# Strassen products of an FFN: 512- and 256-column matmuls in another order, the second kind two k tiles behind the first

## What is computed

```python
def swiglu(h, w_in, w_out):
    a, b = jnp.split(h @ w_in, 2, axis=-1)
    return (jax.nn.silu(a) * b) @ w_out
# h: 512 x 2048, w_in: 2048 x 2*D_FF, D_FF = 5632, all float32
```

## Time and profile before

| | |
|---|---|
| time of the kernel, median of 3 runs | 2776.76 us (2773.27 to 2780.72) |
| the profiled execution's own time | 2771.05 us |
| its span in the profile | 2769.2 us |
| PE busy | 2729.6 us, 99% of the span |
| DVE busy | 2170.0 us, 78% |
| ACT busy | 1140.6 us, 41% |
| granted TensorE clock, mean | 0.997 of full speed |

### The profile page before, as it was taken

The page is one execution under the profiler, slowest core; times in us unless marked ns, Lnnn a source line. Parts: engine busy times, 40 slices in busy tenths (PEclk is TensorE's granted clock), DMA queues, the critical chain, the costliest instruction groups (busy, mean ns, idle before and its releaser), DMA issues.

```text
span 2769.2 us, 39539 instructions
## 1 busy us (share of the span) xinstructions
PE 2729.6 (99%) x15566; PEld 2311.8 (83%) x15566; DVE 2170.0 (78%) x2984; ACT 1140.6 (41%) x1697; POOL 368.5 (13%) x540
## 2 busy tenths in 40 slices
PE   7999999999999999999999999999999999999997
PEld 2688888888888888888888888888888888998996
DVE  6555775987885685676789999999999887877877
ACT  4332333223443532222245555555555554453541
POOL 0001331001333110001100111111111111000001
PEclk9999999999999999999999999999999999999999
DMA  9736885345775645767644444444443336434432
GB/s 403 325 95 148 196 188 144 116 129 191 231 226 180 239 134 182 247 210 269 231 149 145 156 145 149 145 152 144 150 153 125 124 112 217 140 91 148 138 103 96
DMA packets 144540, 475.27 MB, mean 172 GB/s; under 512 B 24993, under 2 KB 29489, under 8 KB 140130
## 3 DMA queue, kind: packets, MB, share of 16 engines
q1 hardware_dynamic: 85858, 301.43, 33.6%
q0 software_dynamic: 49760, 157.67, 18.1%
q10 hardware_dynamic: 8736, 13.63, 1.4%
HBM read 428.14 MB, written 44.44 MB: 171 GB/s over the span
## 4 chain that ended last, share of the span: by engine, by line
PE 92%; DMA 3%; DVE 2%; ACT 2%; issue 0%; SPq 0%; ACTq 0%; POOL 0%; DVEq 0%
PE ps L2831 19%; PE ps L2535 12%; PE ps L2537 12%; PE ps L2536 12%; PE ps L2833 10%; PE ps L2882 3%; PE ps L2881 3%; PE ps L2880 3%; PE ps L2859 2%; PE ps L2860 2%; PE ps L2861 2%; PE ps L2552 2%; DMA ada_mix<-in_w_ac 1%; PE ps L2514 1%; PE ps L2579 1%; PE ps L2621 1%
## 5 line engine op out<-in xcount | busy, mean ns | idle before, releaser
L1407 DVE TENSOR_TENSOR hw_lo<-hw_raw,hw_hi 128x1024 fp32r<-128x1024 f32 x220 | 269.3, 1224 | 318.8 <-ACT hw_hi L868 317.6
L868 ACT ACTIVATE hw_hi<-hw_raw 128x1024 fp32r<-128x1024 f32 x220 | 232.7, 1059 | 674.6 <-DMA hw_raw<-in_w_in 458.3
L2831 PE MATMUL ps<-t_hi_lo,wx_hi 128*128 128x512 f32 x1312 | 412.0, 395 | 0.0
L2103 DVE TENSOR_TENSOR wx_lo<-wx,wx_hi 128x1024 fp32r<-128x1024 f32 x287 | 351.3, 1224 | 41.4 <-ACT wx_hi L1261 36.9
L2535 PE MATMUL ps<-h_hi,hw_hi 128*128 128x512 f32 x896 | 354.0, 395 | 0.0
L2537 PE MATMUL ps<-h_hi,hw_lo 128*128 128x512 f32 x896 | 349.4, 390 | 0.0
L2536 PE MATMUL ps<-h_lo,hw_hi 128*128 128x512 f32 x896 | 348.7, 389 | 0.0
L1261 ACT ACTIVATE wx_hi<-wx 128x1024 fp32r<-128x1024 f32 x287 | 302.8, 1055 | 104.8 <-PE ps L2833 98.9
L2831 PE MATMUL ps<-h_hi_lo,wx_hi 128*128 128x512 f32 x984 | 309.0, 395 | 0.0
L2833 PEld LDWEIGHTS ps<-t_hi_lo,wx_lo 128*128 128x128 f32 x1312 | 246.5, 188 | 58.3
L2833 PE MATMUL ps<-t_hi_lo,wx_lo 128*128 128x256 f32 x1312 | 257.7, 278 | 0.0
(11 more groups left out here) (429 smaller groups left out, 5672.6 us busy)
## 6 DMA issues: line engine op xcount, KB each, us to landing
wx<-in_w_fi SPq DMA_DIRECT2D x164, 512.0 KB, 3.6
hw_raw<-in_w_in SPq DMA_DIRECT2D x128, 512.0 KB, 4.6
ada1m<-in_w_ar POOLq DMA_DIRECT2D x96, 512.0 KB, 4.6
ada_mix<-in_w_ac SPq DMA_DIRECT2D x16, 2048.0 KB, 15.3
dw<-in_w_fo SPq DMA_DIRECT2D x80, 384.0 KB, 3.1
ada1g<-in_w_ar POOLq DMA_DIRECT2D x32, 512.0 KB, 5.2
hw_raw<-in_w_glu SPq DMA_DIRECT2D x32, 512.0 KB, 4.6
hw_raw<-in_w_out SPq DMA_DIRECT2D x32, 512.0 KB, 4.3
```

Source lines behind the costliest of these rows:

```text
L868: act.activation(hw_hi[slot(n)][:, :], hw_raw[slot(n)][:, :], ACT.Copy).then_inc(w_hi, 1)
L1407: tt(hw_lo[s][:, :], hw_raw[s][:, :], hw_hi[s][:, :].bitcast(F32), SUB).then_inc(w_lo, 1)
L2103: tt(wx_lo[b][:, :], wx[b][:, :], wx_hi[o % 4][:, :].bitcast(F32), SUB).then_inc(w_lo, 1)
L2831: mm(out[:, :], wh[:, P * k:P * k + P], both[:, :, k, :], start=opens and k == 0, stop=False, skip_group_check=True)
```

## The change

Before, a product's matmuls stand in groups of two k tiles: two wide, two narrow, and so on. After, the wide matmul of k tile k is followed by the narrow one of k tile k - 2: a product begins with three wide ones, wide and narrow then take turns, and it ends with three narrow ones. No matmul is added or removed and none changes its operands; the waits ahead of the product and the count at its end stay. The order of the additions into a bank is another.

```diff
                 pe.wait_ge(w_lo, N_W + o + 1)
-                for k0 in range(0, ST, 2):
-                    for k in (k0, k0 + 1):
+                for k in range(ST + 2):
+                    if k < ST:
                         mm(out[:, :], wh[:, P * k:P * k + P], both[:, :, k, :], start=opens and k == 0, stop=False, skip_group_check=True)
-                    for k in (k0, k0 + 1):
-                        ins = mm(out[:, 0:CW], wl[:, P * k:P * k + P], xh[:, k, :], start=False, stop=k == ST - 1, skip_group_check=True)
+                    if k >= 2:
+                        ins = mm(out[:, 0:CW], wl[:, P * (k - 2):P * (k - 1)], xh[:, k - 2, :], start=False, stop=k == ST + 1,
+                                 skip_group_check=True)
                 ins.then_inc(w_used, 1)
```

## The result

Over 20 executions of each, the changed kernel took 2781.27 us in the median (2776.14 to 2784.58), the kernel before 2776.12 us (2772.62 to 2781.59). The ratio is 1.0017, with a 95% interval of 1.0011 to 1.0023: 4.7 us slower, clear of the noise and within the 0.3% that the prediction called no change.

What follows compares the result with a forecast made beforehand. TensorE's unbroken matmul sequence was taken as the bound. Couples in turn plus the runs of three gave -2.9 to +6.7 us, +5.5 at 7 to 1, discounted to +4 on 2776.8: 2780.8 us, range 2771 to 2790.

Steps and rivals of the forecast that it cites:

- The bound: Stage of the change, 1491 to 2291 us: TensorE's own matmul sequence sets its length, PE busy all 800.00 us without waiting.
- The size: Whole kernel: +4 us on the median of 2776.8, giving 2780.8 us.
- Five couples in turn, at one of two speeds: Middle of each product: alternating couples at 346.7 or 353.3 ns each, 1733 to 1767 ns for five, 1762 at 7 to 1.
- The share of 7 in 8: Couples in turn in units_by_k and u_half: 7 in 8 ran at 353.3 ns, used to weight the two speeds.
- Three wide and three narrow at 1043.3 ns: Product's start and end: 1040 ns at the unmixed pace plus 3.3 ns for one round trip between the kinds.
- The discount by a quarter: Whole stage: three quarters of +5.5 us taken, +4 us, since the three wide ones restart the sequence in every product.
- The sign that was named in line 2831's length: Wide matmuls of the stage: mean length would rise above 395 ns, towards 397, if turns are slow.
- The weight loads, priced at nothing: Stage: exactly one load lies under each matmul in either order, so the new order costs nothing in load time.
- Free mixing: Rival, 20%: couples in turn run as in u_half's last unit; stage -2.9 us, kernel 2773.9 us.
- The state in which every couple costs 360 ns: Rival, 17%: every turn in the stage is a long one; stage +16 us, kernel 2793 us.
- Cheap narrow ones at 340 ns a couple: Rival, 5%: narrow matmuls slip in at 113 ns behind wide ones; stage 13.4 us less, kernel 2763 us.

Runs made afterwards that it cites:

- e1: Kernel before, each product's eight wide matmuls first, then all eight narrow ones: stage 801.66 us against 799.76, kernel 1.0009 of the kernel before.
- e4: Kernel before, products in the order WWWNNWWWNNNWWNNN (W wide, N narrow), three round trips between the kinds: stage 801.68 us against 799.76.
- e7: Kernel before, wide and narrow in strict turn, narrow matmuls of 192 columns instead of 256: stage 780.61 us.
- e2: Kernel before, wide and narrow matmuls in strict turn from the first k tile: stage 811.24 us against 799.76, kernel 1.0040 of the kernel before.
- e6: Kernel before, wide and narrow in strict turn, narrow matmuls of 384 columns instead of 256: stage 933.70 us.
- e8: Kernel before, with the 16 small matmuls of power_rows one unit of u_half earlier: stage 799.762 us as before, but TensorE waited 5.59 us at them.

## Why the prediction was right, point by point

- **The bound.** Right: TensorE's own sequence sets the stage, before and after, and no wait of PE turned up in it. The loss of 4.5 us is all busy time.
- **The size.** +4 us on the median was forecast; the medians give +5.2, the ratio +4.7 and the stage +4.5. The stage fell within the 796.9 to 806.5 us that were named for it.
- **Five couples in turn, at one of two speeds.** Right in kind: the changed kernel has both, 346.7 ns in one product of three and 351 to 352.5 in the others. Cut as the prediction cut them, from the first narrow matmul to the three last ones, five couples took 1735, 1751 and 1764 ns in the three products of the cycle, 1750 on average, where 1762 was reckoned. The share of 7 in 8 for the slow one was no property of the code. It counted one execution; over 13 traces the fast one is the more frequent in the first three units of u_half.
- **Three wide and three narrow at 1043.3 ns.** This step failed. It took 3.3 ns for a round trip, from four of them costing 13.3, as if each had a price that adds. e1 measured 20 ns for one, and e4 20 for three. In the changed kernel the three wide and three narrow took 1049 to 1055 ns, 1052 on average (in the rows above 0.70 + 0.35 us): 9 ns too few were reckoned here, 12 too many for the couples, and the discount took off another 5. That the sum came out near the measured one (2800.5 after the discount, 2802.2 measured) is luck in that part.
- **The discount by a quarter** for the restart in each product: the mechanism was half right. In one product of three the couples keep the pace of 346.7 ns, so the long turns are not everywhere; but nothing restarts with a product, since the phase is carried on from one to the next.
- **The sign that was named in line 2831's length** failed: its mean stayed at 395 ns. What rose was line 2833's, from 278 to 280. In the stage of each trace a matmul's length in these rows is the distance to the next start plus 159 to 166 ns, so it tells the pace, and not, as the text above has it, when the last result has come out:

```profile
L2831 PE MATMUL ps<-t_hi_lo,wx_hi 128*128 128x512 f32 x1312 | 427.8, 395 | 0.0
L2833 PE MATMUL ps<-t_hi_lo,wx_lo 128*128 128x256 f32 x1312 | 314.0, 280 | 0.0
```

  At full resolution the distance behind a narrow matmul rose from 115.2 to 117.1 ns on average, that behind a wide one from 233.1 to 233.2. So nearly the whole loss, 1.9 ns x 2296 = 4.3 of 4.5 us, stands behind narrow matmuls. In before's order the wide ones were already 6.4 ns over their unmixed 226.7, and the narrow ones 4.8 under their 120.0; the change took away part of that gain. The prediction's sum of both kinds hid this.
- **The weight loads, priced at nothing.** Nothing speaks against it at 256 columns: the loads start with the matmul ahead in either order. With 192 columns one load in two starts late (e7), so the margin may end between the two.
- **The rivals.** Free mixing came true for one product in three. The state in which every couple costs 360 ns never appeared: e2, in strict turn throughout, has 353.3. Cheap narrow ones at 340 ns a couple appeared in none of the 25 orders.
- **What stays open** is what the phase is. The settled values are steps of 6.67 ns over a product or over a cycle of products, and in every order of 512 and 256 columns the wide matmuls are on average further apart than unmixed (229.9 to 236.7 ns) and the narrow ones closer (115.2 to 119.1). Which part of the engine keeps the phase, no run here tells. Nor was it tried to set it on purpose.

## What to carry to other kernels

In a stream of matmuls without a wait, the order of lengths alone moved a stage by 1.7% (797.8 to 811.2 us), and the price did not add up from its parts: measure the whole repeated order, not one change of kind. Many orders can be measured in one execution by giving each a block of identical products, since a block settled within three products and its value held over the whole stage. When the effect is a fraction of a per cent, compare the stage in the trace and not the span, of whose 9.0 us half arose elsewhere. Make sure that the stage repeats: this one did to the nanosecond, while u_half kept one of two paces by execution.

## What the runs showed of the hardware that was not expected

- The same unchanged instructions (u_half) ran at 346.7 or at 353.3 ns a couple, depending on the execution, and kept the pace until the stream was interrupted. For its 192 couples that is 1.3 us of a kernel's scatter.
- Wide matmuls behind eight narrow ones needed 1.84 us for eight, against 1.81 unmixed (e1); the first five ran slower, the last three at the unmixed pace.
- With 192 columns the next load no longer started with the matmul ahead of it but 0.02 us behind, and a couple took 340.0 ns (e7); with 384 columns it took 406.7 (e6), 6.7 over the sum of 226.7 and an estimated 173.3 (halfway between the paces of 256 and 512 columns).
- Behind the 5.59 us of waiting in e8 the granted clock was 0.50, and a couple of 512 and 256 columns in turn took 640 ns, 426 and 214 (346.7 with the clock back at 1.00).
